# Pairing 256-column matmuls into 512-column ones: three output projections and 46 feed-forward items

## The reference, cut to what matters

```python
x = x + 0.5 * rms(swiglu(rms(x)))             # ffn 0
x = x + rms(attention_a_b(rms(x)) @ w_out)    # mixer 0: dense heads and dilated heads
x = x + 0.5 * rms(swiglu(rms(x)))             # ffn 1
x = x + concat(rglru, stick) @ ab_w_out       # mixer 1
x = x + swiglu(rms(x))                        # ffn 2
x = x + concat(s5, moba) @ cd_w_out           # mixer 2
x = x + swiglu(rms(x)); out = rms(x)          # ffn 3
# swiglu(h) = (silu(h @ w_gate) * (h @ w_up)) @ w_down, hidden width 2816
```

## Time and profile before

| | value |
|---|---|
| median of three timed runs | 1105.17 us |
| time of the profiled execution | 1105.69 us |
| its span, first to last instruction | 1103.6 us |
| TensorE busy | 1084.8 us, 98% |
| VectorE busy | 763.2 us, 69% |
| ScalarE busy | 547.7 us, 50% |
| GpSimd busy | 208.3 us, 19% |
| mean granted TensorE clock | 0.997 |
| matmuls of L506 (256 columns) | 3 x 1344 |
| matmuls of L553 (512 columns) | 3 x 336 |
| matmuls of L688 (256 columns) | 3 x 192 |

### The profile page before, as it was taken

The page is one execution under the profiler, slowest core; times in us unless marked ns, Lnnn a source line. Parts: engine busy times, 40 slices in busy tenths (PEclk is TensorE's granted clock), DMA queues, the critical chain, the costliest instruction groups (busy, mean ns, idle before and its releaser), DMA issues.

```text
span 1103.6 us, 21369 instructions
## 1 busy us (share of the span) xinstructions
PE 1084.8 (98%) x8556; PEld 1019.8 (92%) x8556; DVE 763.2 (69%) x1026; ACT 547.7 (50%) x701; POOL 208.3 (19%) x222
## 2 busy tenths in 40 slices
PE   8999999999989999999999999999999999999997
PEld 8999999898989999998999999999999899999996
DVE  5756666886678877666775897666559557666664
ACT  6435434667666344355784643443443555433343
POOL 0006000031059995000000497000000000000000
PEclk9999999999999999999999999999999999999998
DMA  7765445342346654552434655544434235545531
GB/s 255 288 243 198 173 173 200 117 158 77 124 159 233 223 190 171 176 204 97 153 116 153 232 206 194 203 173 173 169 131 170 86 115 207 193 171 190 198 144 38
DMA packets 34976, 189.63 MB, mean 172 GB/s; under 512 B 3824, under 2 KB 4592, under 8 KB 18544
## 3 DMA queue, kind: packets, MB, share of 16 engines
q1 hardware_dynamic: 32624, 181.48, 45.8%
q10 hardware_dynamic: 2016, 6.43, 1.7%
q0 software_dynamic: 288, 1.05, 0.3%
HBM read 187.90 MB, written 1.05 MB: 171 GB/s over the span
## 4 chain that ended last, share of the span: by engine, by line
PE 89%; DVE 5%; ACT 4%; DMA 1%; issue 1%; SPq 0%; ACTq 0%; DVEq 0%
PE ps L506 44%; PE ps L553 21%; PE ps L584 9%; PE ps L688 4%; PE ps L527 2%; DVE gu_low L1624 2%; PE ps L606 1%; DMA gu_raw<-in_wgu 1%; ACT gu_high L1058 1%; PE ps L466 1%; PE ps L639 1%; PE ps L942 1%; PE ps L973 1%; PE ps L670 1%; ACT hT_high L1112 0%
## 5 line engine op out<-in xcount | busy, mean ns | idle before, releaser
L506 PE MATMUL ps<-hT_high,gu_high 128*128 128x256 f32 x1344 | 380.3, 283 | 0.0
L506 PE MATMUL ps<-hT_high,gu_low 128*128 128x256 f32 x1344 | 380.3, 283 | 0.0
L506 PE MATMUL ps<-hT_low,gu_high 128*128 128x256 f32 x1344 | 380.3, 283 | 0.0
L506 PEld LDWEIGHTS ps<-hT_high,gu_high 128*128 128x128 f32 x1344 | 257.7, 192 | 3.4 <-issue 0.3
L506 PEld LDWEIGHTS ps<-hT_low,gu_high 128*128 128x128 f32 x1344 | 257.7, 192 | 3.1
L506 PEld LDWEIGHTS ps<-hT_high,gu_low 128*128 128x128 f32 x1344 | 257.7, 192 | 0.0
L1144 ACT ACTIVATE gu_high<-gu_raw 128x2048 fp32r<-128x2048 f32 x84 | 160.9, 1915 | 122.9 <-PE ps L506 121.8
L1741 DVE TENSOR_TENSOR gu_low<-gu_raw,gu_high 128x2048 fp32r<-128x2048 f32 x83 | 195.7, 2358 | 15.0 <-ACT gu_high L1144 14.9
L1722 DVE TENSOR_TENSOR ffn_s<-scratch,ps 128x256 f32<-128x256 f32 x88 | 36.8, 418 | 159.3 <-PE ps L506 159.3
L1128 ACT ACTIVATE ffn_s<-ffn_s 128x256 f32<-128x256 f32 x88 | 36.8, 418 | 217.1 <-DVE ffn_s L1711 217.0
L1152 ACT ACTIVATE dn_high<-dn_raw 128x1024 fp32r<-128x1024 f32 x84 | 88.9, 1058 | 58.5 <-PE ps L553 58.5
(11 more groups left out here) (318 smaller groups left out, 1901.4 us busy)
## 6 DMA issues: line engine op xcount, KB each, us to landing
gu_raw<-in_wgu SPq DMA_DIRECT2D x126, 1024.0 KB, 4.8
dn_raw<-in_wdn SPq DMA_DIRECT2D x88, 512.0 KB, 5.2
x<-in_x SPq DMA_DIRECT2D x2, 512.0 KB, 5.4
gu_raw<-in_wgu SPq DMA_DIRECT2D x2, 512.0 KB, 6.9
scratch<-in_glu ACTq DMA_DIRECT2D x1, 1024.0 KB, 7.5
scratch<-in_biasM ACTq DMA_DIRECT2D x1, 1024.0 KB, 5.4
out_x<-scratch SPq DMA_DIRECT2D x4, 256.0 KB, 2.6
s5in<-in_s5in ACTq DMA_DIRECT2D x1, 768.0 KB, 4.3
```

What stands on the lines that cost most here:

```text
L506: i = nc.tensor.matmul(bank(4 + 2 * w + h)[:, 0:SEQ], gu[pw_][:, sl, o:o + P], hT[px][:, k, :], start=(pw_, px, k) == (0, 0, 0), stop=(pw_ ...
```

## The change

Three things are done.

1. hT high and low lie side by side in one buffer, for each k 512 contiguous columns. In 46 feed-forward items, named in BOTH, gate_up does the products of the high weights with hT_high and hT_low as one matmul of 512 columns into a whole bank, and the product of the low weights with hT_high as one of 256 columns on top of the first half. Two partial sums then lie side by side in the bank. ScalarE copies the second half out, VectorE adds it to the first half and multiplies by rB in a second instruction: for gate and for up, so two more instructions on each of the two engines in each of these items. TensorE's one loop of a feed-forward part becomes 4, 3, 3 and 2 loops.
2. The items of the output projection hold two units with four chunks of k each instead of one unit with eight. out_unit does 3 matmuls of 512 columns for each chunk. Units 0 and 1 are complete after item 1, units 2 and 3 after item 3. The loads of these 12 items read two pieces of 4 KB for each partition instead of one of 8 KB. wait_bank and the marks mix_t0 and proj_done follow.
3. The order of the calls follows too, and the split of mixer 0's item 2 in two halves goes away. In mixer 0 the order is: chunks 0 to 3 of row half 0, the transposes of pair 7, the values of pair 6, chunks 0 to 3 of row half 1, the values of pair 7, then chunks 4 and 5, 6, and 7 of both row halves.

```diff
+BOTH = (((2, 8), (14, 20)), ((14, 20),), ((10, 20),), ((2, 20),))
...
-        hT = [sb("hT_" + part, [P, KC, SEQ], F32R) for part in ("high", "low")]
+        hT_both = sb("hT", [P, KC, 2, SEQ], F32R)
+        hT = [hT_both[:, :, part, :] for part in range(2)]
...
-                engine.wait_ge(s["proj_done"], UNITS[n] + MIX_IN[n] + 3 if k == 2 else UNITS[n + 1])
+                engine.wait_ge(s["proj_done"], UNITS[n] + MIX_IN[n] + 2 if k == 2 else UNITS[n + 1])
...
+                        u, c = first_out + (g - first_out) // 2 * 2, out_half(m, g - first_out) * 1024
+                        sp_.dma_start(gu_raw[:, slot, :].rearrange("p (u n) -> p u n", u=2),
+                                      a["wgu"][u:u + 2, :, c:c + 1024].rearrange("u p n -> p u n")) \
+                           .then_inc(gu_loaded[slot], 16)
...
+                        out = bank(4 + 2 * w + h)
+                        if both:
+                            nc.tensor.matmul(out, gu[0][:, sl, o:o + P],
+                                             hT_both[:, k, :, :].rearrange("p a s -> p (a s)"),
+                                             start=k == 0, stop=False)
+                            i = nc.tensor.matmul(out[:, 0:SEQ], gu[1][:, sl, o:o + P], hT[0][:, k, :],
+                                                 start=False, stop=k == KC - 1)
+                            continue
...
-                with pe.Fori(1, FCH // 2) as r:
-                    for h in range(2):
-                        gate_up(h, (base + h) % 2, r * 2 + (base + h), r * 2 + (G0 + h))
-                        down(1 - h, r * 2 + (G0 + h - 1))
+                edges = sorted({2, FCH, *(e for pair in BOTH[f] for e in pair)})
+                for first, end in zip(edges, edges[1:]):
+                    with pe.Fori(first // 2, end // 2) as r:
+                        for h in range(2):
+                            gate_up(h, (base + h) % 2, r * 2 + (base + h), r * 2 + (G0 + h), both_at(f, first))
+                            down(1 - h, r * 2 + (G0 + h - 1))
...
+                item, q = MIX_ITEM[m] + MIX_IN[m] + j, j // 2
+                own = 4 * out_half(m, j)
+                pe.wait_ge(s["gu_split"], item + 1)
+                out = bank(2 * t + q).rearrange("p (u n) -> p u n", u=2)
                 for k in ks:
                     pe.wait_ge(*ready(k))
...
+                        both = gu[pw_][:, item % 2, :].rearrange("p (u k n) -> p k u n", u=2, k=4)[:, k - own]
+                        i = nc.tensor.matmul(out, oT[px][:, k, t * P:(t + 1) * P], both,
+                                             start=(pw_, px, k) == (0, 0, own) and j % 2 == 0,
+                                             stop=(pw_, px, k) == (1, 0, own + 3) and j % 2 == 1)
...
-            out_unit(0, 0, 0, early, pair_out)
-            pe.wait_ge(s["ropT_evac"], 7)
-            out_unit(0, 0, 1, early, pair_out)
+            out_unit(0, 0, 0, range(4), pair_out)
             pair_transposes(7)
             pair_values(6)
-            out_unit(0, 1, 0, early, pair_out)
+            pe.wait_ge(s["ropT_evac"], 7)
+            out_unit(0, 0, 1, range(4), pair_out)
             pair_values(7)
...
+                    if both:
+                        act.wait_ge(s["gate_ready"], plain(G0 + 1))
+                        act.wait_ge(s["prod_done"], plain(G0 - 1))
+                        nc.scalar.activation(sil_s[:, h, :], bank(4 + h)[:, SEQ:], ACT.Copy).then_inc(s["gate_rest"], 1)
...
+                    if both:
+                        act.wait_ge(s["up_ready"], plain(G0 + 1))
+                        act.wait_ge(s["act_ready"], plain(G0 - 1))
+                        nc.scalar.activation(prod_s[:, h, :], bank(6 + h)[:, SEQ:], ACT.Copy).then_inc(s["up_rest"], 1)
...
+                        dve.wait_ge(s["gate_rest"], nth)
+                        nc.vector.tensor_tensor(sil_s[:, h, :], gate[:, 0:SEQ], sil_s[:, h, :], ALU.add) \
+                          .then_inc(s["gate_sum"], 1)
+                        dve.wait_ge(s["gate_sum"], nth)
+                        nc.vector.tensor_tensor(sil_s[:, h, :], sil_s[:, h, :], rB[:, :], ALU.mult) \
+                          .then_inc(s["gate_scaled"], 1)
```

More of the change, by code:

```diff
@@ L77, with both_at, both_count, out_half @@
 PAIRS = 8
[L80 to L82 removed]
+ORDER0 = (2, 0, 1, 3, 5, 7, 4, 6, 8)
+ORDER1 = (0, 1, 4, 6, 5, 7, 2, 3, 8, 9)
+ORDER2 = (0, 1, 2, 4, 6, 3, 5, 7)
 HEADS = 4
+BOTH = (((2, 8), (14, 20)), ((14, 20),), ((10, 20),), ((2, 20),))
+def both_at(f, i):
+    return any(first <= i < end for first, end in BOTH[f])
+def both_count(f, i):
+    return sum(min(max((i if g == f else FCH) - first, 0), end - first) for g in range(f + 1) for first, end in BOTH[g])
 ROPES = (2, 0, 1, 3, 5, 4, 6)
 ROPE_AT = (0, 1, 2, 3, 4, 6, 7)
[L86 removed]
+def out_half(m, j):
+    return (j + (m == 2)) % 2
 STICK_Z = (4, 6, 2, 4)
@@ L488, in wait_hT, with gate_up @@
                 pe.wait_ge(s["hT_low"], KC * n + k + 1)
-            def gate_up(h, sl, item, G, first=None, between=None):
+            def gate_up(h, sl, item, G, both=False, first=None, between=None):
                 if first == 0:
@@ L1158, in ffn @@
                 for i in range(2, FCH, 2):
+                    if both_at(f, i) != both_at(f, i - 2) and i > first:
+                        with act.Fori(first // 2, i // 2) as r:
+                            for h in range(2):
+                                step_of(h, r, first)
+                        first = i
                     if i < FCH - 2 and not (side.keys() & {i, i + 1}):
@@ L1752, in ffn @@
                 for i in range(2, FCH, 2):
+                    if both_at(f, i) != both_at(f, i - 2) and i > first:
+                        with dve.Fori(first // 2, i // 2) as r:
+                            for h in range(2):
+                                step_of(h, r, first)
+                        first = i
                     if i < FCH - 2 and not (side.keys() & {i, i + 1}):
```

109 lines of the change are left out of this document (42 added, 67 removed).

## The result

The changed kernel takes 1096.81 us (median of 6 runs, 1095.94 to 1097.46) against 1105.38 (6 runs, 1104.82 to 1106.6): ratio 0.9914, interval 0.9903 to 0.9926. The profiled execution took 1097.15 us, with a span of 1095.3; the spans of both traces differ by 8.3 us and the times of both profiled executions by 8.5. Forecast were 1092.3 us and 12.9 us of gain. So 4 us of it didn't come.

What follows compares the result with a forecast made beforehand. TensorE, busy 98% of the span, was taken as the bound. Items 9.9, mixer 1 2.0, mixer 2 1.35, mixer 0 0, less 0.3 for loops, made 12.9 us: 1092.3 us predicted, range 1090.5 to 1096.

Steps and rivals of the forecast that it cites:

- the price of the pair: Feed-forward items: one 512-column matmul replacing two of 256 saves 13.4 ns; 736 pairs give 9.9 us.
- the join of down and gate_up: Feed-forward items: a 256-column matmul behind a 512-column one costs nothing extra there, within the 8.50 us item.
- the clock: TensorE's granted clock was read at the 2.4 GHz level in all but the last slice; no loss was priced.
- Mixer 0: Output projection of mixer 0: its 1.28 us less work doesn't arrive, gain 0, bounds -0.5 and +0.6 us.
- The new wait: Mixer 0, transposes of head pair 7: TensorE waits 1.5 us for the normalisation on VectorE.
- Mixer 1: Output projection of mixer 1: 1.28 us less work plus a 0.71 us wait gone, gain 2.0 us.
- Mixer 2: Output projection of mixer 2: no new wait, 1.28 us, with small pauses gone 1.35 us.
- Pieces of 4 KB: Loads of the 12 projection items: a landing of 4.8 to 7.4 us costs nothing in mixer 1; price 0 to 1 us.
- The loop entries: Eight more TensorE loop entries at 0 to 0.31 us each, 0 to 2.5 in all; 0.3 us taken.
- VectorE keeps up: The 46 wide items: VectorE follows at 8.29 us per item with some 0.9 us left.
- A: Rival: wide matmul takes 228.7 ns or more and loop entries cost 1.1 us; 1095.3 us, at 233 ns 1099; chance 0.17.

Runs made afterwards that it cites:

- wide_first: Changed kernel with all eight 512-column matmuls of a bank before all eight 256-column ones in the wide items; 1092.64 us, ratio 0.9886.
- two_two: Changed kernel with two wide matmuls and then two narrow ones in turn in the wide items; 1092.0 us beside 1105.41.
- shifted: Changed kernel with the narrow matmul of chunk k behind the wide one of chunk k + 1 instead of its own; 1095.15 us.
- only_ffn: Kernel before with only the wide feed-forward items, output projections as they were; 1099.80 us, ratio 0.9951.
- m0_order: Changed kernel with mixer 0's projection chunks 0 to 3 of both row halves ahead of pair 7's transposes; 1095.85 us.
- only_proj: Kernel before with only the output projections in pairs, no wide feed-forward item; 1103.48 us, ratio 0.9985.
- narrow_second: Changed kernel with the narrow matmul added on the second half of the bank instead of the first; 1096.51 us.
- best_fill: two_two plus m0_order plus mixer 0's bank 2 square and gain moved earlier, with unread matmuls filling TensorE's waits at mixer 0's end; 1091.19 us, ratio 0.9862.

## Why the prediction was off

**The failed step, 4.7 us: the price of the pair.** "I take 13.4 ... A 256-column matmul behind a 512-column one is not in the trace in this form; the join of down and gate_up is ... and it costs nothing extra there." In the projections the wide matmul did come at 226 to 227 ns, so rows 5 was the right row for it there. But that row is a run of wide ones, and in turns a wide and a narrow one take 353 ns (236.4 + 116.9), not 346.3. The pair saves 7.1 ns, not 13.4: 46 x 16 x 7.1 = 5.2 us instead of 9.9. And the witness was misread. The join does cost something, some 20 ns in an item; it sits in the 228.7 ns that the prediction found for down's matmuls and put down to the change of bank. In the same trace the last seven of them change the bank and take 226.7. One join in an item was small; sixteen pairs in turns have no run left. wide_first, two_two and shifted show that it is the order: with two_two the forecast's saving per item (0.21) comes whole, and its one execution, 1092.0 us, lies 0.3 from the forecast for the change.

**The missed term, 1.2 us in the profiled execution: the clock.** The prediction saw the granted clock at its upper level and took it for granted. After the change it fell behind mixer 0, in both traces, although the waits there are those of before. Nothing in the trace of before priced that. One such loss of 1.2 to 1.4 us stands in 7 of the 13 traces of changed kernels. But by the runs' mean clocks it comes and goes with the execution, in the kernel before as well, so it can't be booked as a cost of the change: the 4.5 us between the median and the forecast are no more than the 4.7 of the items.

Between the two traces, 4.7 + 1.2 are 5.9 us too much; short were the start (0.8), mixer 2 (0.2), the loops (0.3), mixer 1 and the end (0.1 each), less 0.25 for mixer 0 and the item behind mixer 1. That is the 4.6 us between 12.9 and 8.3.

**Right:**
- Mixer 0 yields nothing, but the zero is in part luck: 0.5 us of before's 31.33 was a late load, and against only_ffn's 30.82 the change loses 0.6. The new wait measured 1.27 us (1.5 reckoned), the stretch 31.44 us (31.3), and the reason holds: m0_order, which fills the wait, moves gu_high and with it the end by 1.6 us.
- Mixer 1: 2.10 us (2.0), the wait of the earlier trace rows gone and no later one in its place. Mixer 2: 1.57 us (1.35). Both stand unchanged in only_proj.
- Pieces of 4 KB cost nothing: they land in 5.1 us instead of 4.8, inside the 4.8 to 7.4 that the prediction allowed.
- The loop entries cost less than the bound: the parts gain 0.113 us times their items, with nothing left over for one to three entries more.
- VectorE keeps up in the 46 items. Its slack was put at 0.9 us; the like of it measured 1.46. In the items left out the same mechanism costs up to 3.7 + 2.5 = 6.2 us in part 2.

**The rivals.** A named what happened, as one of several causes: the wide matmul is dearer where 256 and 512 columns meet. Its 233 ns (a pair of 353) meets the measured 353 ns, by luck, since no row gave it. But it made the projections and the loop entries dear as well, which they were not, and said 1099. So the time, 1096.8, fell between the forecast and A's dear end and 0.8 us above the range.

**Open:** why wide matmuls behind narrow ones take longer, and whether it is the lone narrow or the lone wide one that counts; why the clock falls behind waits that it survived in the trace of before and in others; the 1.5 us between only_proj's stages and its time.

## What to carry to other kernels

The price of a matmul depends on its neighbours: where widths alternate, group the narrow ones at least in twos, and take the price of a mix from a row that has that mix, or bound it. A wait or a saving that ends behind another chain gives nothing until that chain is moved too, and then all of it (mixer 0: 0, then 1.6 us). A mean over a mixed stretch, like down's 228.7 ns, is to be split by position before it is given a cause. And before an engine with slack is given more work, look for the items in which its neighbour runs: the slack in quiet items says nothing of those.

## What the hardware showed unexpectedly

- 512- and 256-column matmuls in turns cost 6 to 7 ns more for each pair than in runs (353.3 instead of 346.7 ns); two and two cost 1 to 2 (four matmuls 695 ns). PSUM columns and operand don't matter (narrow_second, shifted).
- The first five 512-column matmuls behind a run of 256-column ones last 228 to 236 ns, the rest 226.7, whether or not the bank changes each time.
- The granted clock fell to the 1.2 GHz level for about 3.4 us (1.2 to 1.4 us lost) in 7 of 13 traces of kernels that are 98% busy: four times behind mixer 0, whose last wait is 1.3 us, and three times at the start, behind one of 2.2 to 2.9 us. Nine other traces have the same 1.3 us behind mixer 0 and no loss there.
- VectorE's subtractions of two SBUF operands took up to 3.12 us instead of 2.28, and 2.50 instead of 0.43, beside GpSimd; in before up to 2.83 and 1.22.
- Ahead of mixer 2's projection two traces have an idle time of TensorE with nothing but issue ahead of it (0.78 and 1.31 us, best_fill and only_proj), and that stretch is 1.0 and 1.5 us longer; in two more it is 0.4 and 0.5 us longer.
